# Both ends of a two-layer flow-matching step: modulation weights in column blocks first, the second half finished token by token last

## What is computed

```python
def rms_norm(x, g):
    y = x * lax.rsqrt(jnp.mean(x * x, axis=-1, keepdims=True) + EPS)
    return y * g

# the same for both groups of tokens, w_ada: (2, 1024, 6 * 1024)
mod = silu(c) @ w_ada[layer] + b_ada[layer]
shift1, scale1, gate1, shift2, scale2, gate2 = jnp.split(mod, 6, axis=-1)
h = rms_norm(x, gains[0]) * (1 + scale1) + shift1
x = x + gate1 * rms_norm(mixer(h), gains[1])
h = rms_norm(x, gains[2]) * (1 + scale2) + shift2
x = x + gate2 * rms_norm(jnp.square(relu(h @ w_mlp_in)) @ w_mlp_out, gains[3])
```

## Time and profile before

| | us |
|---|---|
| median of 3 runs | 1740.29 |
| lowest, highest | 1738.31, 1742.33 |
| the profiled execution, its own time | 1740.12 |
| its span | 1738.3 |
| PE busy in it | 1674.2 |
| DVE, ACT, POOL busy in it | 1102.8, 735.0, 213.5 |

### The profile page before, as it was taken

One profiled execution on the slowest core, in us unless ns is written; L12 is line 12 of the kernel. 1 busy time (PEld: TensorE's weight loads), 2 busy tenths in 40 slices (PEclk: granted clock), 3 DMA queues, 4 the chain that ended last, 5 costly groups with the idle time before them and its releaser, 6 DMA issues.

```text
span 1738.3 us, 26413 instructions
## 1 busy us (share of the span) xinstructions
PE 1674.2 (96%) x10650; PEld 1494.3 (86%) x10650; DVE 1102.8 (63%) x1726; ACT 735.0 (42%) x1238; POOL 213.5 (12%) x204
## 2 busy tenths in 40 slices
PE   5999999899999999999999999999999999999997
PEld 3999864689999999999989974445999999999996
DVE  3777666856757777785587647886585653332345
ACT  3433235755653312213345745654475332221333
POOL 0000014432100000000120402443310000000011
PEclk7999999999999999999999989999999999999998
DMA  9455212131556456473412500002154722222231
GB/s 334 155 174 166 82 47 61 29 104 31 149 176 176 121 170 194 122 205 99 116 38 49 149 13 1 1 1 83 52 146 134 206 74 73 73 74 80 79 85 61
DMA packets 266794, 181.63 MB, mean 104 GB/s; under 512 B 26237, under 2 KB 239090, under 8 KB 265650
## 3 DMA queue, kind: packets, MB, share of 16 engines
q1 hardware_dynamic: 266674, 179.96, 35.7%
HBM read 173.75 MB, written 3.62 MB: 102 GB/s over the span
## 4 chain that ended last, share of the span: by engine, by line
PE 81%; DVE 9%; ACT 3%; issue 3%; DMA 2%; SPq 1%; POOL 0%; DVEq 0%; ACTq 0%; POOLq 0%
PE ps L824 21%; PE ps L826 21%; PE ps L825 21%; PE ps L1397 3%; PE ps L1407 2%; DMA ada_a<-in_w_ada 1%; PE ps L990 1%; PE ps L992 1%; PE ps L991 1%; DVE w_lo L575 1%; PE ps L1024 1%; PE ps L1006 1%; PE ps L878 1%; ACT km L1923 1%; ACT w_hi L566 1%
## 5 line engine op out<-in xcount | busy, mean ns | idle before, releaser
L566 ACT ACTIVATE w_hi<-stage 128x1024 fp32r<-128x1024 f32 (+1 forms) x176 | 184.7, 1052 | 615.8 <-PE ps L826 500.1
L575 DVE TENSOR_TENSOR w_lo<-stage,w_hi 128x1024 fp32r<-128x1024 f32 (+1 forms) x176 | 216.8, 1233 | 281.9 <-ACT w_hi L566 281.7
L824 PE MATMUL ps<-hM_hi,w_lo 128*128 128x320 f32 x952 | 295.2, 310 | 0.0
L826 PE MATMUL ps<-hM_hi,w_hi 128*128 128x320 f32 x952 | 294.2, 309 | 0.0
L825 PE MATMUL ps<-hM_lo,w_hi 128*128 128x320 f32 x952 | 294.1, 309 | 0.0
L824 PE MATMUL ps<-h_hi,w_lo 128*128 128x320 f32 x824 | 255.9, 311 | 2.6 <-DVE h_lo L2497 2.6
L826 PE MATMUL ps<-h_hi,w_hi 128*128 128x320 f32 x824 | 254.6, 309 | 0.0
L825 PE MATMUL ps<-h_lo,w_hi 128*128 128x320 f32 x824 | 254.6, 309 | 0.0
L2742 POOL TENSOR_TENSOR rstd<-rstd,sq 128x320 f32<-128x320 f32 x73 | 77.3, 1064 | 960.8 <-ACT sq L1490 959.2
L824 PEld LDWEIGHTS ps<-hM_hi,w_lo 128*128 128x128 f32 x952 | 178.7, 188 | 3.4 <-issue 3.4
L825 PEld LDWEIGHTS ps<-hM_lo,w_hi 128*128 128x128 f32 x952 | 178.7, 188 | 0.1
(11 more groups left out here) (412 smaller groups left out, 3525.8 us busy)
## 6 DMA issues: line engine op xcount, KB each, us to landing
stage<-in_w_mlp_out SPq DMA_DIRECT2D x83, 512.0 KB, 4.2
stage<-in_w_mlp_in SPq DMA_DIRECT2D x80, 512.0 KB, 4.6
slab_mlp<-in_w_ada SPq DMA_DIRECT2D x28, 1024.0 KB, 5.3
stage<-in_w_in_ac SPq DMA_DIRECT2D x28, 512.0 KB, 3.9
slab_ac<-in_w_ada SPq DMA_DIRECT2D x12, 1024.0 KB, 6.1
ada_a<-in_w_ada SPq DMA_DIRECT2D x8, 1024.0 KB, 16.6
stage<-in_w_out_ac SPq DMA_DIRECT2D x8, 512.0 KB, 4.1
stage<-in_w_out_c SPq DMA_DIRECT2D x8, 512.0 KB, 4.3
```

What stands on the lines that cost most here:

```text
L566: nc.scalar.activation(hi_place(n)[:, 0:width], stage[:, n % STAGE, 0:width], ACT.Copy)\
L575: nc.vector.tensor_tensor(lo_place(n)[:, 0:width], stage[:, n % STAGE, 0:width], hi_place(n)[:, 0:width].bitcast(F32), ALU.subtract).then_ ...
L824: mm(out, lo[:, k], xh, start=j == 0, stop=False)
L826: last = mm(out, hi[:, k], xh, start=False, stop=j == k_tiles - 1)
```

## The change

At the beginning:

- The seven small loads are issued by ACT's queue, before its first work. SP begins with `x_sample`, then `x_prompt`, then the weights of shift and scale in four column blocks q of 256 columns each of shift and scale (tiles 2q and 2q + 1), 2 MB each, in two transfers with runs of 1 KB: block 0, pieces 0 and 1, block 1, piece 2, blocks 2 and 3, piece 3. SP issues the first two slabs behind a wait for the last modulation step (`ada_done`), since they now share memory with the blocks; pieces 4 and on come behind them.
- `ada_step(q)` is 32 matmuls of 128 columns (8 row tiles, 4 groups). Each block has its own row copy, turn and `first_columns(q)`. The spread inverse roots are copied by ACT from PSUM to SBUF.
- PE makes, block by block, the products of tiles 2q and 2q + 1 for both halves, with the next step between the halves. Block 0 is for units 0 and 1, block 1 for units 0 to 2 and, for unit 2, the tiles 0 and 1 too.
- The second half's low parts are formed by POOL instead of DVE.
- Token turns use eight PSUM banks instead of four.

At the end:

- The first half's finished tiles stay in `xT`, and PE turns them during the sweeps 11 to 14 of `down13` (8 tiles, 3 blocks each). The gated tiles of the second half are turned, one sweep after their own, during sweeps 9 to 15 and the last behind them. ACT copies each to `ytok` and `gtok`.
- Behind the last product PE turns the second half of `xT` into PSUM, 24 transposes, and sums the squares with the tokens on the partitions, six matmuls of one column. ACT takes three roots of one column, DVE three reciprocals, and then six operations of 512 columns: gated tile times the token's factor, plus x.
- A store is a block of tokens with whole rows of 4 KB; the first half's three are issued during the sweeps, and one of the last three by ACT's queue.

The core of the diff:

```diff
-ADA_START = 1
+ADA_START = 4
+ADA_Q = 256
...
-            for k in range(KD):
-                sp.dma_start(ada_a[:, k, :], i["w_ada"][0, P * k:P * (k + 1), 0:4 * GRP]).then_inc(ada_in[k], 16)
...
+            load_ada(0)
+            load_piece("ac", 0)
+            load_piece("ac", 1)
+            load_ada(1)
+            load_piece("ac", 2)
+            load_ada(2)
+            load_ada(3)
+            load_piece("ac", 3)
...
+            sp.wait_ge(ada_done, ADA_START)
             load_slab(0)
             load_slab(1)
...
+            def ada_step(q):
+                pe.wait_ge(ada_in[q], 32)
+                if q >= 2:
+                    pe.wait_ge(mod_out, q - 1)
+                for k in range(KD):
+                    for j in range(4):
+                        last = mm(ps[32 * j:32 * j + 32, 4 + q % 2, 0:P], cwide[:, k, :], ada_a[:, q, k, P * j:P * (j + 1)],
+                                  start=k == 0, stop=k == KD - 1)
+                last.then_inc(ada_done, 1)
...
+            def tile_products(k, part, units):
                 pe.wait_ge(w_lo_done, units[-1] + 1)
+                h_ready("in0", part)(k, k)
...
+            ada_step(0)
+            turn_modulation(0)
+            spread_rows(0)
+            spread_rows(1)
...
+            for q in range(ADA_START):
+                units = (0, 1, 2) if q else (0, 1)
+                for part in range(2):
+                    tile_products(2 * q, part, units)
+                    if part and q < ADA_START - 1:
+                        turn_modulation(q + 1)
+                    tile_products(2 * q + 1, part, units)
+                    if q == 1:
+                        tile_products(0, part, (2,))
+                        tile_products(1, part, (2,))
+                    if part == 0 and q < ADA_START - 1:
+                        ada_step(q + 1)
```

ACT's and DVE's order at the beginning:

```diff
+            modulation_row(0)
+            spread_copy(0)
+            spread_copy(1)
+            for q in range(ADA_START):
+                if q in (0, 1):
+                    act_split(act, 2 * q)
+                for s in range(2):
+                    operand("in0", s, 2 * q)
+                    operand("in0", s, 2 * q + 1)
+                    if s == 0 and q == 0:
+                        act_split(act, 1)
+                if q < ADA_START - 1:
+                    modulation_row(q + 1)
+            act_split(act, 3)
...
+            for q in range(ADA_START):
+                first_columns(q)
+                k = 2 * q
                 modulate("in0", 0, k)
+                modulate("in0", 0, k + 1)
+                if q == 0:
+                    dve_split(dve, 0)
+                low("in0", 0, k)
+                low("in0", 0, k + 1)
                 modulate("in0", 1, k)
+                modulate("in0", 1, k + 1)
+                if q == 0:
+                    dve_split(dve, 1)
+                if q == 1:
+                    dve_split(dve, 2)
+            dve_split(dve, 3)
```

The end, PE and DVE:

```diff
+            def late_beside(u):
+                v, after = u - 8, {}
+                if v == 0:
+                    after[3] = lambda: sum_squares("y1m", 0)
+                if 3 <= v < 7:
+                    after[2] = lambda: late_turn("first", 2 * v - 6)
+                    after[4] = lambda: late_turn("first", 2 * v - 5)
+                if v:
+                    after[6] = lambda: late_turn("g", v - 1)
+                return after
...
+            late_tokens(0)
+            token_sums()
+            late_turn("g", KD - 1)
+            late_tokens(1)
+            late_tokens(2)
...
+            for b in range(3):
+                rows = slice(0, token_count(1, b))
+                dve.wait_ge(x_t, 10 + b + 1)
+                for n in (1, 0):
+                    dve.wait_ge(y_out, len(late) - n)
+                    cols = slice(512 * n, 512 * (n + 1))
+                    stt(gtok[rows, b, cols], gtok[rows, b, cols], rs[rows, 0, b:b + 1], ps[rows, x_banks[b][n], :],
+                        ALU.mult, ALU.add).then_inc(xN_done, 1)
```

More of the change, by code:

```diff
@@ L600, in build, with token_block, token_count, late_before @@
         o_lo = [x[:, T:2 * T] for x in o_tiles]
[L602 to L608, removed]
+        def token_block(tile, s, b):
+            return tile[:, (0, P, 2 * P)[b]:(P, 2 * P, HALF)[b]] if s == 0 else tile[:, (0, P, 3 * HD)[b]:(P, 3 * HD, HALF)[b]]
+        def token_count(s, b):
+            return (P, P, HD)[b] if s == 0 else (P, HD, P)[b]
+        late = []
+        for v in range(KD):
+            if 3 <= v < 7:
+                late += [("first", 2 * v - 6), ("first", 2 * v - 5)]
+            if v:
+                late.append(("g", v - 1))
+        late.append(("g", KD - 1))
+        late_bank = {(kind, k): (1 if kind == "first" else 6) + (2 if kind == "first" else 1) * (k % 2) for kind, k in late}
+        x_banks = ((1, 3), (0, 2), (4, 6))
+        def late_before(kind, k):
+            n = late.index((kind, k))
+            return [m + 1 for m in range(n) if late_bank[late[m]] == late_bank[kind, k]][-1:]
         spare = stage[:, 2:4, :].rearrange("p n c -> p (n c)")
@@ L1186, in project_out, with late_turn @@
                          beside=sums_beside(f"y{layer}a", f"in{layer}m", 0, 4, u - 8))
+            def late_turn(kind, k):
+                n = late.index((kind, k))
+                for count in late_before(kind, k):
+                    pe.wait_ge(y_out, count)
+                if kind == "first":
+                    pe.wait_ge(xN_first, k + 1)
+                    tile, s = xT[:, k, 0:HALF], 0
+                else:
+                    pe.wait_ge(gy_done, k + 1)
+                    tile, s = gy[:, SECOND["down13"][k], :], 1
+                for b in range(3):
+                    last = nc.tensor.transpose(ps[0:token_count(s, b), late_bank[kind, k], P * b:P * (b + 1)],
+                                               token_block(tile, s, b), ident[:])
+                last.then_inc(y_t, 1)
@@ new lines, in token_sums @@
+            def token_sums():
+                at, n = NORM_AT["y1m"], NORM_K["y1m"]
+                parts = [(rstd[:, half(1)], False), (sq[:, (n - 1) % 2, half(1)], True)]
+                pe.wait_ge(added[1], ADD_AT["y1m"] + n - DIRECT["y1m"])
+                pe.wait_ge(sq_done[1], at + n)
+                for b in range(3):
+                    for k, (tile, end) in enumerate(parts):
+                        last = mm(ps[0:token_count(1, b), 5, b:b + 1], token_block(tile, 1, b), ones[:, 0:1],
+                                  start=k == 0, stop=end)
+                last.then_inc(sums_done[1], 1)
@@ L1781, in gated_tile, with late_copy, late_copies @@
                 last.then_inc(gy_done, 1)
+            def late_copy(kind, k):
+                n, bank = late.index((kind, k)), late_bank[kind, k]
+                act.wait_ge(y_t, n + 1)
+                s, place, j = {"first": (0, ytok, k), "g": (1, gtok, SECOND["down13"][k])}[kind]
+                for b in range(3):
+                    rows = token_count(s, b)
+                    last = f(place[0:rows, b, P * j:P * (j + 1)], ps[0:rows, bank, P * b:P * (b + 1)], ACT.Copy)
+                last.then_inc(y_out, 1)
+            def late_copies(u):
+                v = u - 8
+                if 3 <= v < 7:
+                    late_copy("first", 2 * v - 6)
+                    late_copy("first", 2 * v - 5)
+                if v:
+                    late_copy("g", v - 1)
             def mlp(layer):
```

272 lines of the change are left out of this document (125 added, 147 removed).

## The result

The changed kernel takes 1743.30 us (median of 12 runs, 1740.17 to 1745.63) against 1739.85 (12 runs, 1737.36 to 1742.63) of the kernel before on the same chip: ratio **1.0021, 95% interval 1.0013 to 1.0028**. It is 3.5 us slower; forecast was 1738.1, a gain of 2. The median lies inside the range (1732.5 to 1744.5), and the direction is wrong. The profiled run took 1743.28 us, with a span of 1741.3; the span before was 1738.3, so the two traces differ by 3.0 us.

A forecast was written before the change was run, and what follows sets the result against it. TensorE was taken as the bound from its first dense work to its last product. Tail -8.8, end transposes +5.0 and beginning +1.8 sum to -2.0 us against 1740.12: 1738.1 us, range 1732.5 to 1744.5.

The forecast's parts named there:

- x and its turn: At the start: sample load lands at 8.7 us with small loads on ScalarE's queue, and x is turned at 17.6.
- A modulation step: At the beginning: each step of 32 matmuls takes 2.5 us, between bounds of 1.9 and 7.5.
- the slower rival: Modulation steps: records do not shrink with their columns, 5.0 us a step, kernel 1748.1 us; chance 0.15.
- First product: At the beginning: TensorE's first product at 28.8 us instead of 41.0, 12.2 earlier.
- Clock: At the beginning: TensorE idles from 22.95 to 28.8, so products start at 1.2 GHz for 5 us.
- "no change" rival: Transposes at 0.18 us, or a second clock fall before block 1 costing 2.5: 1741.1 or 1740.6; no separate chance.
- The wait for piece 2: Before block 1: TensorE waits 4.1 us, until 41.3, for VectorE's split of piece 2.
- Products end: End of block 3's products for units 0 to 2: at 66.1 us, against 66.0 before.
- From there to unit 3: After those products: ScalarE evacuates as before, pieces 4 and 5 arrive by 65.5 and 67.1, unit 3 starts at 68.65.
- The beginning loses 1.8: Whole beginning: unit 4 starts at 76.6 instead of 74.85, everything behind moves along, 1.8 us lost.
- The end on PE: Last eight sweeps: 45 added transposes at 0.11 us each make TensorE 5.0 us later.
- The tail: Behind the last product: 11.3 us instead of 20.3, 9.0 won, 8.8 with a wait; last store 2.9 to 3.4.

The follow-up runs named there:

- Number 7: Changed kernel with modulation bias and two short gains loaded by GpSimd instead of ScalarE; first product 29.32 instead of 30.36, first milestone 0.36 us earlier.
- Number 4: Changed kernel with ScalarE and VectorE splitting weight piece 2 at the end of block 0's work; ratio 0.9991 to the kernel before.
- number 5: Changed kernel, pieces 4 and 5 loaded before SyncE's wait, units 0 and 1 evacuated before splits, VectorE's piece 4 split earlier; 2.6 us shorter than changed kernel.
- number 6: Changed kernel with the edits of number 4 and number 5 together; ratio 0.9985 to the kernel before.
- number 10: Number 9 with the last three stores cut into six halves, issued by SyncE and ScalarE in turn; ratio 0.9977 to the kernel before.
- number 9: Kernel before with the new end, ScalarE's two evacuations before its splits, VectorE's piece 4 split one slot earlier; 1733.31 us, ratio 0.9972.
- number 3: Changed kernel with 34 idle transposes in TensorE's wait before block 1 and 28 in that before unit 3; 1740.85 us.

## Why the prediction was wrong

By its own steps, in their order:

- **x and its turn.** The prediction had x at 8.7 and turned at 17.6; x came at 8.9 and was turned at 19.8. It had put the seven small loads on ScalarE's queue at the cost of their issue alone. The last of them, issued at 3.68, took 6.2 us to land, beside x's 2 MB, and VectorE's short chain of the small rows then stood in front of its copies. Number 7 moved that one away and won 1.0 of the 2.2 us; there the gains, still on ScalarE's queue, came last.
- **No block waited for.** Right; the 1 KB pieces moved at about 347 GB/s.
- **A modulation step**, 2.5: the four took 1.96, 2.56, 1.95 and 1.95, the longest partly at the lower clock. The low end of the bounds was true, 64 records in 1.96 us, 31 ns each. The 1.6 us that the four steps saved against the forecast hide as much of what went wrong elsewhere. The Trainium skill (TensorE: Matmul & The Clock Gate, the section on the HAM clock gate) gives 62 ns for every matmul where the sequencer works without hardware decoding. By that a step would have taken an estimated 4.0 us, and the slower rival would have come true. The 31 ns of this trace are not that case.
- **First product**, 28.8: 30.36, later by the 2.2 us that x was late, less what the step saved.
- **Clock.** The first fall came as forecast. A second in the wait for piece 2 was priced and set aside as part of the "no change" rival; it came, for 1.4 us. A third one behind unit 3's wait was not seen at all, another 1.4.
- **The wait for piece 2**, 4.1: it was 3.9, in its place. The prediction accepted it as a property of the order. Number 4 shows that one moved split wins 3.8 us, the clock behind the wait included.
- **Products end**, 66.1: about 68.2, the late start and the second fall less what the steps saved.
- **From there to unit 3**, the step that failed most plainly. "Both just in time" (65.5 and 67.1): piece 5 landed at 69.82. Of these 2.7 us, 1.9 came from modulation step 3, which ended at 58.2 instead of 56.35 and so let SyncE go on late, and 0.8 from the transfers: the two slabs and both pieces, issued from 58.27 on behind SyncE's added wait, took 11.6 us. ScalarE had that piece's split in front of the evacuation which freed PE's accumulator. I had written "as before" for an order whose cover, transfers long done, was what the change removed. Unit 3 came 3.0 us later than forecast, and its clock loss, 1.4, is added to that. VectorE's bound, from which the forecast of unit 4 was taken (76.6), came at 78.5 and was not what unit 4 waited for: 3.0 and 1.4 more, less the 0.9 that the bound had been given, put unit 4 at 80.1 instead.
- **The beginning loses 1.8**: it lost 5.4. This term is the error: 3.6 of the 5.0 us between the forecast sum (-2.0) and the traces (+3.0). The two waits behind it, repaired, give back 3.8 and 3.05 us at the first milestone (numbers 4 to 6).
- **The end on PE**, 5.0: 5.2, and 4.94 when doubled. The row of four such transposes priced it well, and no gated tile was waited for.
- **The tail**, 9.0 won: 8.0. The engines' chain was 0.5 shorter than forecast; the last store ended 4.8 us behind its issue where 3.4 had been taken. That price came from a single store; here three were issued within 2.6 us, and number 10, with smaller stores spread out, ended its last one after 4.0.
- The rest, 0.4, is gathered between the milestones.

Of the rivals none came true as written; the result is the second half of "no change", enlarged. The beginning is not bound by modulation weights once they come in columns: it then runs through four rounds of row, turn, columns, operands and split, and with both repairs it starts the later work no earlier than the old order with its own wait mended (-1.45 against -2.02 and -0.99). The 10.6 us by which products begin sooner are spent again before unit 3: PE is idle there for 8.9 us instead of 1.8, and has 6.5 us of modulation steps and 0.8 of turns between its products.

## What to carry to other kernels

When work is moved forward, go through every wait that "was there before" and ask whether its cover moved too; here the evacuation behind a split behind a transfer was harmless only while the transfer was early. A wait on PE can cost more than its length: the two of 3.9 and 3.2 us each cost another 1.4 us in slow products behind them, so it is worth placing a split or an evacuation by hand. Find a distinct instruction common to both kernels and compare at that, before stretches whose clock varies: at the first milestone kernels with the same beginning differed by up to 1 us, at the end of the sweeps, counted from the third milestone, by 0.01, while the clock in the middle moved whole spans by up to 4.5.

## What the runs showed of the hardware

**The clock in the middle of the kernel is not the same in every trace.** Between 950 and 1170 all kernels run the same instructions, and their offsets change there by +0.3 to -4.5 us. The tables by stretch of the kernel before and of number 9 show where:

```profile
1015.00:1025.00 10.00, 7.72 (x44) 6.62 (x43) 6.25 (x11) 3.87 (x8) 0.00 (x0) 0.87 0.00 0
1025.00:1035.00 10.00, 9.72 (x51) 8.75 (x51) 2.93 (x5) 6.19 (x10) 0.00 (x0) 0.50 0.01 2
```
```profile
1015.00:1025.00 10.00, 7.45 (x43) 6.28 (x42) 5.52 (x10) 5.74 (x11) 0.00 (x0) 0.81 0.00 0
1025.00:1035.00 10.00, 9.89 (x96) 9.12 (x97) 2.14 (x4) 6.90 (x11) 0.00 (x0) 0.85 0.01 2
```

From 1025 the kernel before stays at the lower level for all 10 us, number 9 for 3. Over the 50 us from 1015, five such rows each, the time at the lower level comes to 20.4 us in the one and 13.6 in the other; half of the difference, 3.4, is about what number 9's offset changes by (-1.70 at 950, -4.69 after). So 3 us of the lead that its profiled run shows come from there, as much as the new end is worth. All thirteen traces fit this. Of the 60 us from 1010, the clock is 0.83 in the kernel before and in six others, whose offsets change by -0.2 to +0.3 between the last two milestones; it is 0.89 in five, which win 2.5 to 3.0; and 0.94 in number 5, which wins 4.5:

```profile
1010.00:1070.00 60.00, 52.60 (x268) 36.57 (x266) 33.05 (x51) 29.40 (x52) 7.80 (x8) 0.83 0.00 1
```
```profile
1010.00:1070.00 60.00, 50.93 (x289) 34.82 (x288) 34.76 (x53) 31.30 (x56) 7.77 (x8) 0.94 0.00 1
```

A kernel differs from itself in the same way: of number 6's 11 timed runs the shortest, 1730.50, has a mean granted clock of 0.992, the longest, 1739.19, of 0.984. So a single trace tells little of a whole span, and ratios rest on many runs. Why the clock falls in one run and not in another was not tried. The Trainium skill (TensorE: Matmul & The Clock Gate, the section on the HAM clock gate) says that the number of slow matmuls at a kernel's start changes from run to run; here something like it is seen in the middle.

**Transposes kept the clock up.** In number 3 nothing but transposes ran for 3.9 and 3.2 us, and the clock behind them was 1.00. In every trace that left PE idle there, the clock fell within the wait or right behind it: in four traces with the 3.9 us, in four with the 3.2. The Trainium skill (TensorE: Matmul & The Clock Gate, the section on the PE-mode transpose) says that the full clock does not engage for transpose-mode matmuls, as they don't count as busy in the same way. The rows call these MATMUL against the identity and do not tell the mode; in the form that the kernel issues, they kept the clock at its higher level.

**A small load beside a large one takes about 6 us.** The 48 KB bias landed 6.2 us after its issue at 3.68, beside the 2 MB of x, and 5.7 us after it when issued at 1.27 from another queue.
